# The head of a two-block kernel: squares shared by ScalarE and VectorE, five buffers summed in PSUM, low chunks with waits of their own

## What is computed

```python
def rms_norm(x, w):
    xf = x.astype(jnp.float32)
    y = xf * lax.rsqrt(jnp.mean(xf * xf, axis=-1, keepdims=True) + EPS)
    return (y * w.astype(jnp.float32)).astype(x.dtype)
def modulate(h, shift, scale):
    return h * (1.0 + scale[:, None, :]) + shift[:, None, :]
def swiglu(h, w1, w3, w2):
    return (jax.nn.silu(h @ w1) * (h @ w3)) @ w2
...
        m_l = jnp.split(cond_lat @ ada_w[i] + ada_b[i], N_MOD, axis=-1)
        m_c = jnp.split(cond_ctx @ ada_w[i] + ada_b[i], N_MOD, axis=-1)
        x = x + 0.5 * m_l[2][:, None, :] * swiglu(modulate(rms_norm(x, norm1_w[i]), m_l[0], m_l[1]), ...)
        ctx = ctx + 0.5 * m_c[2][:, None, :] * swiglu(modulate(rms_norm(ctx, norm1_w[i]), m_c[0], m_c[1]), ...)
```

## Time and profile before

| what | value |
|---|---|
| median of 3 runs | 1977.63 us (1974.81 to 1978.48) |
| the profiled execution | 1975.45 us |
| its span | 1973.7 us |
| TensorE busy | 1938.0 us, 98% |
| VectorE, ScalarE, GpSimd busy | 988.2, 825.6, 899.4 us |
| mean granted clock of TensorE | 0.997 |

### The profile page before, as it was taken

One profiled execution on the slowest core, in us unless ns is written; L12 is line 12 of the kernel. 1 busy time (PEld: TensorE's weight loads), 2 busy tenths in 40 slices (PEclk: granted clock), 3 DMA queues, 4 the chain that ended last, 5 costly groups with the idle time before them and its releaser, 6 DMA issues.

```text
span 1973.7 us, 26305 instructions
## 1 busy us (share of the span) xinstructions
PE 1938.0 (98%) x9614; PEld 1630.6 (83%) x9614; DVE 988.2 (50%) x1443; ACT 825.6 (42%) x1281; POOL 899.4 (46%) x640
## 2 busy tenths in 40 slices
PE   9999999999999999889999999999999999999998
PEld 7999999999988885557888888877855878888887
DVE  6888877657456206865313112368954552112123
ACT  6325243334355234563322224457575453222231
POOL 1457565656524322453454454645632345353542
PEclk9999999999999999999999999999999999999999
DMA  8234343433312121002232332332221123232321
GB/s 355 106 110 177 108 156 121 151 130 128 118 55 85 54 73 43 22 22 91 86 106 86 106 106 85 107 139 75 96 75 53 65 75 107 85 107 85 107 85 65
DMA packets 54497, 197.71 MB, mean 100 GB/s; under 512 B 6176, under 2 KB 8832, under 8 KB 52608
## 3 DMA queue, kind: packets, MB, share of 16 engines
q1 hardware_dynamic: 53248, 191.47, 27.6%
q10 hardware_dynamic: 1152, 4.92, 0.7%
HBM read 194.27 MB, written 2.10 MB: 99 GB/s over the span
## 4 chain that ended last, share of the span: by engine, by line
PE 91%; DVE 5%; ACT 2%; issue 1%; DMA 1%; POOL 0%; SPq 0%; DVEq 0%; ACTq 0%; POOLq 0%
PE ps L2482 48%; PE ps L2664 13%; PE ps L2701 8%; PE ps L2496 3%; PE ps L3319 2%; PE ps L2471 2%; PE ps L2469 2%; PE ps L2470 2%; PE ps L2936 1%; PE ps L2927 1%; DVE ada_prod L1541 1%; PE ps L2596 1%; PE ps L2999 1%; PE ps L3117 1%; DMA raw<-panels 1%
## 5 line engine op out<-in xcount | busy, mean ns | idle before, releaser
L702 POOL TENSOR_TENSOR wlo<-raw,whi 128x512 fp32r<-128x512 f32 x488 | 669.5, 1399 | 872.2 <-ACT whi L756 845.3
L756 ACT ACTIVATE whi<-raw 128x1024 fp32r<-128x1024 f32 x244 | 253.7, 1053 | 266.3 <-PE ps L2482 169.0
L2482 PE MATMUL ps<-h_hi,whi 128*128 128x512 f32 (+2 forms) x952 | 351.0, 384 | 0.0
L2482 PE MATMUL ps<-h_hi,wlo 128*128 128x512 f32 (+2 forms) x952 | 347.5, 380 | 0.0
L2482 PE MATMUL ps<-h_lo,whi 128*128 128x512 f32 (+2 forms) x952 | 346.9, 379 | 0.0
L710 POOL TENSOR_TENSOR wlo<-raw,whi 128x512 fp32r<-128x512 f32 x108 | 160.4, 1500 | 121.8 <-ACT whi L934 121.3
L2482 PEld LDWEIGHTS ps<-h_hi,whi 128*128 128x128 f32 x952 | 175.1, 188 | 34.5 <-issue 1.9
L2482 PEld LDWEIGHTS ps<-h_lo,whi 128*128 128x128 f32 x952 | 174.7, 188 | 34.1 <-issue 1.9
L2482 PEld LDWEIGHTS ps<-h_hi,wlo 128*128 128x128 f32 x952 | 174.8, 188 | 32.5
L2482 PE MATMUL ps<-g_hi,whi 128*128 128x512 f32 (+1 forms) x440 | 169.6, 386 | 0.0
L2482 PE MATMUL ps<-g_lo,whi 128*128 128x512 f32 (+1 forms) x440 | 169.5, 385 | 0.0
(11 more groups left out here) (498 smaller groups left out, 3678.8 us busy)
## 6 DMA issues: line engine op xcount, KB each, us to landing
raw<-panels SPq DMA_DIRECT2D x280, 512.0 KB, 3.2
ada_w<-ada_t SPq DMA_DIRECT2D x56, 512.0 KB, 3.8
ada_f<-ada_p SPq DMA_DIRECT2D x8, 1024.0 KB, 19.8
x_lat<-x_t SPq DMA_DIRECT2D x2, 1024.0 KB, 6.7
out<-x_lat SPq DMA_DIRECT2D x16, 128.0 KB, 1.9
x_ctx<-ctx_t SPq DMA_DIRECT2D x2, 512.0 KB, 7.6
cond_b<-cond SPq DMA_DIRECT2D x1, 1024.0 KB, 27.6
x_ctx<-mem_t ACTq DMA_DIRECT2D x1, 1024.0 KB, 4.7
```

The costliest lines, as they stand in the source:

```text
L702: ins = pool.tensor_tensor(wlo[:, sl], raw[:, sl], whi[:, sl].bitcast(f32), ALU.subtract)
L756: act.activation(whi[:, sl], raw[:, sl], ACT.Copy).then_inc(hi_done, 1)
L2482: ins = pe.matmul(bank(banks + b, n), wt[:, w], a[:, at_(kc, c0):at_(kc, c0) + n], start=kc == k_start and j == 0, stop=kc == n_k - 1 and ...
```

## The change

ScalarE now squares chunks 0, 1, 4, 5, 6 and VectorE chunks 3, 2, 7, each into a buffer of its own. VectorE makes three sums only: 0 + 1, 7 + 4, 5 + 6. TensorE adds up five buffers (3, 2, 0 + 1, 7 + 4, 5 + 6) as columns in one PSUM bank, into which a product with zeros has been written first, in the order in which they come. The fillers are 8 and 1 instead of 22, 6 and 1. The log-sigmoids are split in two: the second part stands behind the sums and before the reciprocal. Modulation columns 0 come before the spread, modulation rows 2 go into the first chunk of the loop. In the loop, the passes go high, low weight, low activation, for both panels each, with a wait for `hhi_done` ahead of the first and for `h_ready` ahead of the last; modulation columns and rows stand between them. VectorE makes the low part of chunk 0 before it turns to chunk 1. ScalarE copies the modulation rows after `h32`, not before it. `normed` and `low` are the bodies of the former loop of VectorE's `norm`, taken out as functions with the same instructions.

```diff
@@ -246,6 +246,8 @@
+        first_sq = {0: act_a[:, 0:TOK], 1: act_a[:, TOK:2 * TOK], 2: prod[:, TOK:2 * TOK], 3: prod[:, 0:TOK]}
+        first_sq.update({kc: at(f"first_sq{kc}", TOK, (R_HI, R_LO)[kc // 2 % 2] + (8 + 3 * (kc % 2)) * KB)[:, :] for kc in range(4, KC)})
@@ -762,16 +764,40 @@
             def square(m, kc):
-                if m.n == 0:
-                    act.wait_ge(x_loaded[kc // (KC // 2)], 32)
-                else:
-                    act.wait_ge(down_evac, x_final(m.n) + kc + 1)
+                act.wait_ge(down_evac, x_final(m.n) + kc + 1)
                 if kc >= 3:
...
+            def first_squares():
+                for kc in (0, 1, 4, 5, 6):
+                    act.wait_ge(x_loaded[kc // (KC // 2)], 32)
+                    for xs, n, c0, _ in norms[0].segs():
+                        ins = act.activation(first_sq[kc][:, c0:c0 + n], xs[:, kc * n:(kc + 1) * n], ACT.Square)
+                    ins.then_inc(sq_ready, 1 if kc < 6 else KC - 4)
+            def first_norm(m):
+                act.wait_ge(stats_ready, 1)
+                act.activation(rms[:, 0:TILES], bank(3, TILES), ACT.Sqrt, bias=eps_t).then_inc(root_ready, 1)
+                round_panel(1, 1)
+                modulation_row(1)
+                for kc in range(KC):
+                    act.wait_ge(xn_ready, kc + 1)
+                    b = (kc % 2) * TOK
+                    for j, (_, n, c0, _) in enumerate(m.segs()):
+                        ins = act.activation(h_hi[:, m.at(kc, c0):m.at(kc, c0) + n], prod[:, b + c0:b + c0 + n], ACT.Identity, bias=m.B[j](kc))
+                    ins.then_inc(hhi_done, 1)
+                    for j, (_, n, c0, _) in enumerate(m.segs()):
+                        ins = act.activation(h32[kc][:, c0:c0 + n], prod[:, b + c0:b + c0 + n], ACT.Identity, bias=m.B[j](kc))
+                    ins.then_inc(h32_done, 1)
+                    if kc + 2 < KC:
+                        modulation_row(kc + 2)
+                    if kc in (KC - 3, KC - 2):
+                        round_panel(kc - 3, 1)
@@ -842,10 +868,6 @@
-                if m.n == 0:
-                    modulation_row(0)
-                    round_panel(1, 1)
-                    modulation_row(1)
@@ -858,14 +880,6 @@
-                    if m.n == 0:
-                        if kc + 2 < KC:
-                            modulation_row(kc + 2)
-                        for j, (_, n, c0, _) in enumerate(m.segs()):
-                            ins = act.activation(h32[kc][:, c0:c0 + n], prod[:, b + c0:b + c0 + n], ACT.Identity, bias=m.B[j](kc))
-                        ins.then_inc(h32_done, 1)
-                    if m.n == 0 and kc in (KC - 3, KC - 2):
-                        round_panel(kc - 3, 1)
@@ -1475,10 +1489,10 @@
-            for kc in range(KC):
-                square(norms[0], kc)
+            first_squares()
             round_panel(0, 1)
-            norm(norms[0])
+            modulation_row(0)
+            first_norm(norms[0])
@@ -1565,6 +1579,27 @@
+            def first_sums():
+                def squared(kc):
+                    dve.wait_ge(x_loaded[kc // (KC // 2)], 32)
+                    for xs, n, c0, _ in norms[0].segs():
+                        x = xs[:, kc * n:(kc + 1) * n]
+                        ins = dve.tensor_tensor(first_sq[kc][:, c0:c0 + n], x, x, ALU.mult)
+                    ins.then_inc(sum_done, 1)
+                def added(a, b, n_squares, n_sums, by):
+                    dve.wait_ge(sq_ready, n_squares)
+                    dve.wait_ge(sum_done, n_sums)
+                    dve.tensor_tensor(first_sq[a], first_sq[a], first_sq[b], ALU.add).then_inc(sum_done, by)
+                squared(3)
+                squared(2)
+                added(0, 1, 2, 2, 1)
+                squared(7)
+                added(7, 4, 3, 4, 1)
+                added(5, 6, KC, 5, 2)
@@ -1627,36 +1662,49 @@
...
+            def first_norm(m):
+                token_factors(m)
+                modulation(0)
+                dve.wait_ge(rstd_ready, 1)
+                normed(m, 0)
+                low(m, 0)
+                for kc in range(1, KC + 1):
+                    if kc < KC:
+                        modulation(kc)
+                        if kc >= 2:
                             dve.wait_ge(h32_done, kc - 1)
-                        for j, (xs, n, c0, _) in enumerate(m.segs()):
-                            o = xs[:, kc * n:(kc + 1) * n] if m.last else prod[:, b + c0:b + c0 + n]
-                            ins = dve.scalar_tensor_tensor(o, xs[:, kc * n:(kc + 1) * n], m.A[j](kc), bank(6 + j, n),
-                                                           ALU.mult, ALU.mult)
-                        ins.then_inc(xn_ready, 1)
-                    if kc > 0 and not m.last:
-                        k = kc - 1
-                        b = (k % 2) * TOK
-                        dve.wait_ge(hhi_done, H_BEFORE[m.n] + k + 1)
-                        dve.wait_ge(xn_ready, m.xn0 + k + 1)
-                        for j, (_, n, c0, _) in enumerate(m.segs()):
-                            sl = slice(m.at(k, c0), m.at(k, c0) + n)
-                            src = prod[:, b + c0:b + c0 + n]
-                            if m.B is None:
-                                ins = dve.tensor_tensor(h_lo[:, sl], src, h_hi[:, sl].bitcast(f32), ALU.subtract)
-                            else:
-                                ins = dve.scalar_tensor_tensor(h_lo[:, sl], src, m.B[j](k), h_hi[:, sl].bitcast(f32),
-                                                               ALU.add, ALU.subtract)
-                        ins.then_inc(h_ready, 1)
-                        dve.wait_ge(h_ready, H_BEFORE[m.n] + k + 1)
+                        normed(m, kc)
+                    if kc > 1:
+                        low(m, kc - 1)
...
@@ -1957,9 +2004,18 @@
-                for k in (13, 11, 9, 7, 5, 3, 1):
+                series((13, 11))
+            def series(ks):
+                w2, p = ls_tmp[:, 32:48], ls_tmp[:, 48:64]
+                for k in ks:
                     link(dve.tensor_tensor(p, p, w2, ALU.mult))
                     link(dve.tensor_scalar(p, p, 1.0 / k, None, ALU.add))
+            def log_sigmoids_ended():
+                w, p = ls_tmp[:, 16:32], ls_tmp[:, 48:64]
+                series((9, 7, 5, 3, 1))
@@ -2411,11 +2467,11 @@
-            log_sigmoids()
+            log_sigmoids_begun()
             dve.sem_inc(ada_used, 2 * ADA_PE)
-            for kc in range(1, KC):
-                add_squares(norms[0], kc)
-            norm(norms[0])
+            first_sums()
+            log_sigmoids_ended()
+            first_norm(norms[0])
@@ -2549,7 +2605,7 @@
-                    out = bank(2 * t + 1, 1) if m.apart else bank(5, 1, 64 + t) if m.n == 0 else bank(4, 1, t)
+                    out = bank(2 * t + 1, 1) if m.apart else bank(4, 1, t)
@@ -2599,36 +2655,59 @@
-                keep_busy(0, 22)
+                keep_busy(0, 8)
                 pe.wait_ge(condt_ready, 1)
+                pe.matmul(bank(3, TILES), ident, zero_t.broadcast_to([P, TILES]), start=True, stop=False, skip_group_check=True)
+                first_means(3, 1)
+                first_means(2, 2)
+                first_means(0, 3)
+                keep_busy(0, 1)
+                first_means(7, 5)
                 modulation_rows(0)
-                keep_busy(0, 6)
-                norm_means(norms[0])
-                keep_busy(0, 1)
-                norm_spread(norms[0])
+                first_means(5, KC - 1).then_inc(stats_ready, 1)
                 pe.wait_ge(sel_ready, 1)
                 modulation_columns(0)
+                norm_spread(norms[0])
                 modulation_rows(1)
                 modulation_columns(1)
-                modulation_rows(2)
                 for kc in range(KC):
-                    if kc + 2 < KC:
-                        modulation_columns(kc + 2)
-                    if kc and kc + 3 < KC:
-                        modulation_rows(kc + 3)
+                    pe.wait_ge(hhi_done, kc + 1)
+                    for c in range(2):
+                        if kc == 0:
+                            pe.wait_ge(hi_done, c + 1)
+                        first_pass(kc, c, whi, h_hi)
+                    if kc == 0:
+                        modulation_rows(2)
                     for c in range(2):
                         if kc == 0:
                             pe.wait_ge(lo_done, c + 1)
-                        pe.wait_ge(h_ready, kc + 1)
-                        w = slice(c * PANEL + kc * P, c * PANEL + (kc + 1) * P)
-                        for j, (wt, a) in enumerate(((whi, h_hi), (whi, h_lo), (wlo, h_hi))):
-                            for b, c0, n in halves(TOK):
-                                ins = pe.matmul(bank(2 * c + b, n), wt[:, w], a[:, hidden_at(kc, c0):hidden_at(kc, c0) + n],
-                                                start=kc == 0 and j == 0, stop=kc == KC - 1 and j == 2)
```

(60 more changed lines are left out.)

## The result

The changed kernel takes 1984.16 us (median of 6 runs, 1980.53 to 1986.43) where the kernel before takes 1976.23 (6 runs, 1974.81 to 1978.48): ratio 1.0034, 95% interval 1.0024 to 1.0045 (the ratio is estimated over all runs and isn't the quotient of the two medians). That is slower by more than 0.2%, +7.9 us where I forecast +1.2, and above the range. The profiled execution took 1986.43 (span 1984.6), 10.9 of span more than the one before.

The account below looks back on a forecast made before the run. TensorE, busy 98% of the span, was taken as the bound: first pass +0.3, loop 26.8 against 26.26, half clock in the first chunk +0.3, together +1.2 us, giving 1978.8 us, range 1973.5 to 1982.5.

Parts of the forecast that it names:

- The squares: Square sums in the head, split over ScalarE and VectorE: last sum ends at 15.45 us, 1.7 us sooner than before.
- The clock: TensorE's granted clock in the head: at 1.2 GHz from about 11 us on, since the filler is cut.
- The tail: Log-sigmoid instructions before the reciprocal: about 3 us, held twice by GpSimd to 20.3, hidden while the sums are late.
- uncovered it would be held four times: Rival at whole clock: GpSimd holds the tail four times, reciprocal at 22.0, no change, 1977.7 us; chance 0.14.
- what VectorE wins is lost in TensorE's queue: Column sums in the head: last group ends at 20.9 us against 19.3 before, 1.6 us late despite sooner squares.
- a one-column group at 1.2 GHz: Column sums at half clock: each group taken as 1.77 times its full-clock time, bounds 1.0 and 2.0.
- the first fillers: Shortened filler matmuls at the kernel's start: slow at 0.41 us a record, taken to end at 7.9 us.
- The loop: First pass to panel 2: 26.8 us against 26.26 before, cadence 3.65 kept, plus 0.3 for half clock.
- TensorE's two waits with their refill: Loop waits of 0.5 before columns and 0.57 before the last chunk: taken as gone, 1.2 us off with refill.
- the slower rival: Half clock outlasts the first chunk, to about 33 us: +4.2 us, 1981.8 us and more; chance 0.13.
- dips that had dense work in them: Earlier clock falls at 555 to 560 and 820 to 825 us, some three us each, used to size the half clock.
- I let a shift go through whole.: Behind the head: a shift of panel 2's start, 52.29 us before, reaches the kernel's end unchanged.

Follow-up runs that it names:

- e5: The change with two column-summed buffers instead of five (ScalarE squares six chunks, VectorE two) and more fillers, against the kernel before: ratio 1.0028.
- e4: The change with TensorE's wait in the first layer's down products split per two banks, against the kernel before: 1.0018, 1980.63 us against 1977.59.
- e10: The change itself run once more, unchanged, on another experiment's chip, against the kernel before: ratio 1.0025.
- e2: The kernel before with only the change's loop (TensorE, ScalarE, VectorE), against the kernel before: ratio 1.0008, not told from no change.
- e1: The change's front and log-sigmoid tail with the loop of before, against the kernel before: ratio 1.0031, +6.0 us.
- e12: The kernel before with the change's loop, but passes ordered high, low activation, low weight, against the kernel before: ratio 1.001.
- e3: The change with filler matmuls between the column sums, before the spread and before the first pass, against the kernel before: ratio 1.0048.

## Why the prediction was wrong, by its steps

**Right.** The squares: last sum ends at 15.45, as forecast. The clock: down from 11.28, forecast "from about 11 us on". The tail: held twice, done at 20.3, covered; uncovered it would be held four times with the reciprocal at about 22.0, and e5 measured four holds and 23.2. The direction, and that what VectorE wins is lost in TensorE's queue: the gain of 1.7 on the sums became 22.8 - 19.3 = 3.5 of loss behind the column groups.

**Mis-sized: a one-column group at 1.2 GHz.** I took 1.77 times the full-clock time, by the spread; three groups measured 2.56, 2.70 and 2.72 against 1.25 to 1.40, so 2.0 times, my upper bound. The last group ends at 22.8, not 20.9, and the first pass starts at 28.40, not 26.35, 2.05 late. These three groups are 1.0 of it. The pair of chunks 3 and 2, which ended at 12.16 and not 11.7, is 0.5, and filler and modulation rows at half clock are 0.3 more; the rest lies behind the last group. One more size was wrong at no cost: the first fillers ended at 6.6, not 7.9, so that TensorE waited 2.35 before the first group.

**Mis-sized: the loop.** Forecast 26.8 and 0.3 for half clock, measured 29.0, so 1.9 more. Half clock made 1.5 of it (it lasted to 31.76), not 0.3 of bounds 0 to 1.7, and the reorder itself is 27.5 - 26.8 = 0.7 longer than forecast (e4, e10, without half clock in the loop). I had taken off TensorE's two waits with their refill, 1.2; a wait of 0.56 for the low chunk is still there, at 54.47, and the cadence is 3.73 (41.25 to 44.98), not 3.65. e2 agrees, with a loop of 29.0 and half clock for 3.4 of it. Together panel 2 was at 57.4, not 53.5. This is in substance the slower rival, half clock to some 33 us and +4.2, to which I gave 0.13: its place was the right one, its chance too small. The term that drove it, the time at half clock, varies by 7 us between two profiles of this kernel (13.65 and 20.48), and I had sized it from dips that had dense work in them.

**The step that failed: "I let a shift go through whole."** I read it from the earlier trace rows as: panels, casts and VectorE's queue all hang on the head's last chunk. But the change moves VectorE's last low chunk by more than panel 2 (the low pass is now the last one of a chunk, so that VectorE starts the chunk only 2.15 us ahead of panel 2, not 3.42), and 70 us behind it stands a wait whose end follows VectorE. There 5.1 became 7.7 (1.3 more by that order and 1.3 more by the slow load), the wait grew from 1.27 to 2.86, and the clock fell at it: 2.8 more. e10 shows the same in smaller (2.58, a fall of 3.4 us), e1, e12 and e4 the converse (1.55, 1.44 and 1.53, no fall). e2 had 2.20 and no fall, e5 2.16 and one, so the length of the wait alone does not decide it, and what else does stays open. I never looked for the next wait of TensorE behind the head, although the trace of before has one between 60 and 140 us. A shift of 5 us that went through whole would have been 1982.7, just above my range.

**The Trainium skill.** "TensorE: Matmul & The Clock Gate" ("HAM oscillation — how this bites in real kernels") says that waits between bursts start the next burst at half rate. The 2.86 before 128.02, with 0.50 from its last 0.7 us on, agrees. The 2.35 before 9.04 agrees less well: the burst behind it began at the whole clock, which fell at 11.28. That section speaks of gaps only, and e3 adds that without any gap (5.00 of 5) the clock was 0.50 among one-column groups. The Trainium skill's "SBUF — State Buffer" ("Who interferes with whom") counts `tensor_scalar` too among those that can meet GpSimd at the shared ports, under conditions on its operands; the 16-column TENSOR_SCALAR of 1.14 for 0.17 at 16.82 agrees, while that part of the tail was named in my sum only as "tiny instructions".

## What to carry to other kernels

Work taken off one engine and given to TensorE as one-column matmuls is dear where it replaces filler: count it at twice its time if the clock can fall, look at the granted clock and not at the busy share, and keep wide fillers around it. When a change moves a start, list every wait of the bounding engine behind it and ask which engine's chain ends each; a shift of that other engine, and not of the bound, sets what comes back, and a fall of the clock at a wait that has grown can cost as much again (2.86 of wait, 2.8 behind it). An instruction that is covered today (the tail) is the next bound as soon as the cover goes, so move it off the path in the same edit.

## What the runs showed of the hardware

- One-column matmuls count as TensorE's busy time, and the clock fell among them with no gap: 5.00 of 5 us busy at 0.50 (e3, 15 to 20 us, half of it one such group). A group of six took 1.40 at the full clock and 2.55 to 2.72 at half.
- The same kernel was at half clock in the head for 20.5 us in one profile and 13.7 in another, with the last two column groups at the same times; e1 had 23.9. So single profiles of such a kernel differ by some 5 us (1986.43 and 1981.45), and only medians compare.
- One GpSimd instruction of 1.25 us held a VectorE instruction on 16 columns of SBUF for 1.14 to 1.20, whether it had one tensor input or two; e5 has four such holds beside four GpSimd instructions, 4.7 us for 0.7 us of work.
- The load of one 512 KB weight panel, issued at the same place of the same kernel, took 7.87 us in one profile and 6.11 in another (the change, e10); the difference came through to TensorE's wait 20 us later, less 0.5.
